# Two neighbouring up slots as one 2 MB transfer, with 16 KB in each partition

## The reference

```
logits = h @ w_router + b_router                # 32 experts, top 4 of each token
gates  = softmax(top values)
# for every block of rows that belong to one expert e:
gu   = xb @ w_up[e] + b_up[e]                   # w_up[e]: 1024 x 2048, 8 MB
gate = minimum(gu[:, :1024], 7);  up = clip(gu[:, 1024:], -7, 7)
act  = (up + 1) * (gate * sigmoid(1.702 * gate))
out  = act @ w_down[e] + b_down[e]              # w_down[e]: 1024 x 1024, 4 MB
y    = sum over the token's experts of gate weight * out
```

## Time and profile before

| | |
|---|---|
| time, median of 3 | 1277.09 us (1276.79 to 1278.07) |
| time of the profiled execution | 1276.55 us |
| its span, first to last instruction | 1274.8 us |
| granted TensorE clock, mean | 0.984 |
| PE busy | 1155.6 us (91%) |
| POOL busy | 650.7 us (51%) |
| DVE busy | 540.6 us (42%) |
| ACT busy | 242.6 us (19%) |
| HBM read | 447.00 MB, 353 GB/s over the span |

### The profile page before, as it was taken

The page is one execution under the profiler, slowest core; times in us unless marked ns, Lnnn a source line. Parts: engine busy times, 40 slices in busy tenths (PEclk is TensorE's granted clock), DMA queues, the critical chain, the costliest instruction groups (busy, mean ns, idle before and its releaser), DMA issues.

```text
span 1274.8 us, 30490 instructions
## 1 busy us (share of the span) xinstructions
PE 1155.6 (91%) x11113; PEld 578.5 (45%) x11114; DVE 540.6 (42%) x1161; ACT 242.6 (19%) x483; POOL 650.7 (51%) x743
## 2 busy tenths in 40 slices
PE   8999999999999889888898998998988889889886
PEld 7877777775434333333233433333333333333232
DVE  1999984122633233433332343332333233323424
ACT  2012124000222122122122221221212111222122
POOL 0022300000566766857862678577576765756863
PEclk9999999999999999999999999998999999999998
DMA  9983433642899999999998999999999999999993
GB/s 261 341 272 109 135 131 135 264 168 101 354 422 402 422 421 422 422 422 421 422 422 374 367 407 422 422 422 422 422 415 422 422 422 422 421 422 422 422 421 153
DMA packets 94581, 449.06 MB, mean 352 GB/s; under 512 B 8526, under 2 KB 42894, under 8 KB 45339
## 3 DMA queue, kind: packets, MB, share of 16 engines
q1 hardware_dynamic: 79918, 345.88, 68.1%
q0 software_dynamic: 13872, 101.52, 19.3%
q10 hardware_dynamic: 749, 1.19, 0.3%
HBM read 447.00 MB, written 2.42 MB: 353 GB/s over the span
## 4 chain that ended last, share of the span: by engine, by line
PE 41%; DMA 27%; DVE 13%; POOL 8%; issue 8%; POOLq 1%; ACT 1%; DVEq 0%; SPq 0%; ACTq 0%
DMA ring<-in_w_down 19%; PE banks L1392 13%; DVE arena L815 8%; DMA arena<-in_w_up 8%; PE banks L1405 8%; PE banks L1190 8%; POOL ring L526 7%; PE banks L1105 3%; PE banks L1306 2%; PE banks L1170 2%; PE banks L1142 2%; PE banks L1179 1%; PE banks L1149 1%; POOL ring L528 1%; DVE arena L824 1%
## 5 line engine op out<-in xcount | busy, mean ns | idle before, releaser
L1392 PE MATMUL banks<-ring,hT 128*32 128x512 f32 x3328 | 419.2, 603 | 44.6 <-POOL ring L528 32.9
L526 POOL COPY ring<-arena 128x1024 f32<-128x1024 f32 x279 | 291.2, 1044 | 129.8 <-POOLq L520 127.4
L528 POOL COPY ring<-arena 128x1024 f32<-128x1024 f32 x279 | 292.6, 1049 | 36.9 <-POOL ring L526 0.9
L1405 PE MATMUL banks<-ring,hT 128*32 128x256 f32 x3328 | 224.4, 389 | 45.2 <-DMA ring<-in_w_down 44.9
L345 DVE TENSOR_TENSOR xq<-xq,banks 128x256 f32<-128x256 f32 x53 | 22.3, 421 | 500.7 <-PE banks L1179 500.7
L1392 PEld LDWEIGHTS banks<-ring,hT 128*32 128x32 f32 x3328 | 98.2, 110 | 203.6 <-issue 96.4
L1190 PE MATMUL banks<-hT,ring 128*128 128x288 f32 x768 | 190.5, 409 | 0.0
L1405 PEld LDWEIGHTS banks<-ring,hT 128*32 128x32 f32 x3328 | 101.3, 111 | 185.8 <-issue 78.6
L532 POOL DMA_DIRECT2D ring<-in_w_down x96 | 50.8, 529 | 257.3 <-POOLq L520 142.6
L1190 PEld LDWEIGHTS banks<-hT,ring 128*128 128x128 f32 x768 | 146.4, 192 | 40.2
L783 DVE TENSOR_SCALAR WT<-slot_ids,prod 128x128 f32 x153 | 86.6, 622 | 62.3 <-PE banks L1105 62.0
(11 more groups left out here) (250 smaller groups left out, 817.1 us busy)
## 6 DMA issues: line engine op xcount, KB each, us to landing
arena<-in_w_up SPq DMA_DIRECT2D x248, 1024.0 KB, 14.1
ring<-in_w_down POOLq DMA_DIRECT2D x96, 1024.0 KB, 11.4
arena<-in_w_down SPq DMA_DIRECT2D x31, 1024.0 KB, 16.2
ring<-in_w_in SPq DMA_DIRECT2D x24, 1024.0 KB, 10.2
ring<-in_w_up SPq DMA_DIRECT2D x8, 1024.0 KB, 4.8
ring<-in_w_branch_b SPq DMA_DIRECT2D x4, 1024.0 KB, 4.9
ring<-in_w_branch_a SPq DMA_DIRECT2D x4, 1024.0 KB, 4.8
ring<-in_w_out SPq DMA_DIRECT2D x4, 1024.0 KB, 4.9
```

Of the source, the lines that this page charges most:

```text
L526: nc.gpsimd.tensor_copy(ring[:, k, 0:D], parked[k][:, 0:D]).then_inc(half_copied, 1)
L528: nc.gpsimd.tensor_copy(ring[:, k, D:SLOT], parked[k][:, D:SLOT]).then_inc(slot_full[k], 16)
L1392: ins = mm(UP[g * BLK:(g + 1) * BLK, :], xT[:, k, :], ring[:, k, g * 512:(g + 1) * 512], start=k == 0, stop=k == UP_SLOTS - 1)
L1405: ins = mm(DN[q * BLK:(q + 1) * BLK, 0:256], actT[:, f % 4, f // 4, :], ring[:, UP_SLOTS + j, h * D + q * 256:h * D + (q + 1) * 256], star ...
```

## The change

Up slots 2j and 2j+1 are loaded by one transfer. The 256 rows of w_up that they cover are dealt out so that partition p gets rows 2p and 2p+1, which are neighbours in HBM: 16 KB in one piece. Before, partition p of slot k got row p of its 128, 8 KB. The first row of each pair lies in the even slot, the second in the odd one. So the rows of the contraction that belong to an even slot are the even ones of the 256, and the token rows are turned by every second column (`pairs` in `turn_rows`). The norm weights are needed in this order too: a second copy of `norm_ffn_g` is loaded as four rows of 256, turned by two small transposes at the start into `pair_cols`, and used in `take_x`.

A pair has one semaphore, that of its even slot. SP loads a pair again when POOL has copied its odd slot. POOL's copies of both slots wait for the landing of the pair. The down slots are loaded as before.

```diff
+        def up_pair(e, k):
+            return a["w_up"][0, bass.ds(e, 1), k * P:(k + 2) * P, :].rearrange("e (p h) n -> p (e h n)", p=P)
...
-            def load_parked_again(place, after, ks):
-                for k in ks:
-                    sp.wait_ge(slot_full[k], place * 16 + 16 * FILLS)
-                    load_parked(after, k)
+            def load_parked_pair(e, k):
+                sp.dma_start(arena[:, k * SLOT:(k + 2) * SLOT], up_pair(e, k)).then_inc(parked_full[k], 16)
...
-            for k in range(EARLY_SLOTS):
-                load_parked(1, k)
-            for k in range(UP_SLOTS):
+            for k in (0, 2):
+                load_parked_pair(1, k)
+            for k in range(0, UP_SLOTS, 2):
                 sp.wait_ge(*mix_block_used(MIX_BLOCKS - SLOTS + k))
-                load_slot(0, k)
-                if k == 3:
-                    load_parked(1, EARLY_SLOTS)
+                sp.wait_ge(*mix_block_used(MIX_BLOCKS - SLOTS + k + 1))
+                load_pair(0, k)
+                if k == 2:
+                    load_parked_pair(1, 4)
...
             with sp.Fori(1, NE - 1) as place:
-                load_parked_again(place + 1, after, STAGED)
+                for k in range(0, UP_SLOTS, 2):
+                    sp.wait_ge(slot_full[k + 1], place * 16 + 16 * FILLS)
+                    load_parked_pair(after, k)
+                sp.wait_ge(slot_full[UP_SLOTS], place * 16 + 16 * (FILLS + 1))
+                load_parked(after, UP_SLOTS)
...
-                pool.wait_ge(parked_full[k], 16 * e)
+                pool.wait_ge(parked_full[k - k % 2 if k < UP_SLOTS else k], 16 * e)
...
+            act.dma_start(ws_region[0:4], a["norm_ffn_g"][0].rearrange("(j n) -> j n", j=4)).then_inc(vec_in, 16)
...
-                V.tensor_tensor(xT, XB[:, 256:512].rearrange("p (k t) -> p k t", k=KC),
-                                cols[:, NORM_FFN, :].unsqueeze(2).to_broadcast([P, KC, BLK]), ALU.mult
+                V.tensor_tensor(xT.rearrange("p (j h) t -> p j h t", h=2),
+                                XB[:, 256:512].rearrange("p (j h t) -> p j h t", j=4, h=2),
+                                pair_cols.unsqueeze(3).to_broadcast([P, 4, 2, BLK]), ALU.mult
...
-                    pe.wait_ge(vec_in, 16 * 8)
+                    pe.wait_ge(vec_in, 16 * 9)
+                    for h in range(2):
+                        tr(bank[7][:, 384 + 4 * h:388 + 4 * h], pair_rows[:, h])
...
+                pairs = xg.rearrange("t (p h) -> t h p", h=2)
                 for h in range(2):
-                    ins = tr(turned[:, h], xg[:, h * P:(h + 1) * P])
+                    ins = tr(turned[:, h], pairs[:, h])
...
             def up(k, fills):
-                pe.wait_ge(slot_full[k], fills)
+                pe.wait_ge(slot_full[k], fills - 16 * (k % 2))
```

More of the change, by code:

```diff
@@ L110, in hybrid_layer @@
         slot_ids = sb("slot_ids", [P, MAX_ROUNDS * BLK + BLK])
-        cols = sb("cols", [P, 8, KC])
+        cols = sb("cols", [P, 9, KC])
         bupT = sb("bupT", [P, NE, 2 * KC])
@@ L143, in hybrid_layer @@
         tmpc = region(2 * T).rearrange("p (h t) -> p h t", h=2)
-        WS = region(G * NS)[0:NS].rearrange("p (g i) -> p g i", g=G)
+        ws_region = region(G * NS)
+        WS = ws_region[0:NS].rearrange("p (g i) -> p g i", g=G)
+        pair_rows = ws_region[0:4].rearrange("j (p h) -> j h p", h=2)
         glu_tail = region(KC * NS).rearrange("p (c t) -> p c t", c=KC)
@@ L284, in hybrid_layer @@
         NORM_MIX, GATE_A, GATE_B, B_B, CONV_B, LNC_G, LNC_B, NORM_FFN = range(8)
+        pair_cols = cols[:, 8, :].rearrange("p (h j) -> p j h", h=2)
         vec_names = ["norm_mix_g", "b_gate_a", "b_gate_b", "b_branch_b", "conv_b", "ln_conv_g",
@@ L405, in load_slot, with load_pair @@
                 sp.dma_start(ring[:, k, :], weights(e, k)).then_inc(slot_full[k], 16)
+            def load_pair(e, k):
+                sp.dma_start(ring[:, k:k + 2, :].rearrange("p s n -> p (s n)"), up_pair(e, k)).then_inc(slot_full[k], 16)
             def load_parked(e, k):
                 sp.dma_start(parked[k], weights(e, k)).then_inc(parked_full[k], 16)
-            def load_parked_again(place, after, ks):
-                for k in ks:
-                    sp.wait_ge(slot_full[k], place * 16 + 16 * FILLS)
-                    load_parked(after, k)
+            def load_parked_pair(e, k):
+                sp.dma_start(arena[:, k * SLOT:(k + 2) * SLOT], up_pair(e, k)).then_inc(parked_full[k], 16)
             sp.wait_ge(sp_evac, 2 * G)
             sp.wait_ge(v_stored, 16)
-            for k in range(EARLY_SLOTS):
-                load_parked(1, k)
-            for k in range(UP_SLOTS):
+            for k in (0, 2):
+                load_parked_pair(1, k)
+            for k in range(0, UP_SLOTS, 2):
                 sp.wait_ge(*mix_block_used(MIX_BLOCKS - SLOTS + k))
-                load_slot(0, k)
-                if k == 3:
-                    load_parked(1, EARLY_SLOTS)
+                sp.wait_ge(*mix_block_used(MIX_BLOCKS - SLOTS + k + 1))
+                load_pair(0, k)
+                if k == 2:
+                    load_parked_pair(1, 4)
             sp.wait_ge(ya_evac, 2 * KC)
-            for k in range(EARLY_SLOTS + 1, PARKED - 1):
-                load_parked(1, k)
+            load_parked_pair(1, 6)
             sp.wait_ge(*mix_block_used(MIX_BLOCKS - SLOTS + UP_SLOTS))
             load_slot(0, UP_SLOTS)
-            load_parked(1, PARKED - 1)
+            load_parked(1, UP_SLOTS)
             sp.wait_ge(before_known, 1)
@@ L739, in _ @@
                     dve.wait_ge(pe_early, 1)
-                    V.tensor_copy(cols[:].rearrange("p v c -> p (v c)"), bank[7][:, 320:320 + 8 * KC]
+                    V.tensor_copy(cols[:].rearrange("p v c -> p (v c)"), bank[7][:, 320:320 + 9 * KC]
                                   ).then_inc(evac_early, 1)
```

## The result

| | before | after |
|---|---|---|
| time, median (lowest to highest) | 1276.94 us (1275.13 to 1278.07), 4 runs | 1319.91 us (1318.56 to 1321.28), 4 runs |
| ratio, 95% interval | | 1.0337 (1.0321 to 1.0353) |
| span of the profiled execution | 1274.8 us | 1317.4 us |

The change makes the kernel 43 us slower. The forecast was 54 us slower, 1331 us. The two spans differ by 42.6 us, and this is what the rest accounts for. Lines have moved: the up product is now L1410, the down product L1423, POOL's two half copies L539 and L541.

What follows compares the result with a forecast made beforehand. The prediction took the DMA engines to pace the expert loop, with PE waiting at the down product for slot 11's direct transfer. 1276.55 + 64.8 - 12.5 + 2.2 = 1331 us, range 1308 to 1345 (0.60); 8 in 10: 1282 to 1345.

Steps and rivals of the forecast that it cites:

- What bounds the kernel: Expert loop: DMA engines set the pace; PE waits 44.9 us at the down product for direct transfers, slot 11's last.
- The gain of a large piece: Up weights on SP's queue: 16 KB takes 611.7 ns against 621.2 for two of 8 KB, 0.30 us per expert.
- The loss of the other queue: POOL's direct transfers, in turn with 16 KB pieces, land 7.2 us later at nine places: 64.8 us.
- SP's queue doesn't run dry: During the direct transfers, SP's 4.4 MB open at 529 us and its next loads keep q1 busy over the 22 us.
- half of it: Rival: SP's queue runs dry in part of the nine places, 22 us slower, 1299 us (1284 to 1308); chance 0.13.
- The tenth place left out: Last long wait before the gap at 698 us: SP's open loads run out, so no 7.2 us counted there.
- What is given back: Short waits of 2.30 us at the down product, seven times, a body after the long ones, go: 12.5 us.
- The later issue: A pair's even slot is requested 2.2 us later: 2.2 us paid at the first reload, four other places taken at 0.
- The small parts: Strided turns, permuted output of `take_x` (0 to 4.4 us, taken at 0), and under 0.5 us at the start.
- The waits: Sign of being right: long waits of about 10 us at the down product and no short ones.
- The larger piece wins: Rival: engines share bytes evenly, 9.1 us off over 30 experts, 1272 us, 1267 at best; chance 0.12.
- Pieces of 8 KB: Rival: hardware cuts the pieces to 8 KB, leaving only the later issue, 1279 to 1290 us; chance 0.10.

Runs made afterwards that it cites:

- e12: Kernel before with slots 10 and 11 as one direct 2 MB transfer in 16 KB pieces, up slots still loaded singly in 8 KB pieces; 1273.18 us, ratio 0.9969.
- e1: Changed kernel with each 2 MB pair transfer in 8 KB pieces and the old order of rows; 1288.93 us, ratio 1.0085.
- e3: Kernel before with POOL's direct transfers cut into 4 KB pieces, SP's side untouched; 1340.3 us, ratio 1.05.
- e6: Changed kernel with SP's load of slot 8 cut into 4 KB pieces; 1294.54 us, ratio 1.0139.
- e10: Changed kernel's rows, but only slots 4 to 7 loaded as pairs in 16 KB pieces, slots 0 to 3 singly in 8 KB; 1310.79 us, ratio 1.0267.
- e8: Kernel before with the single loads of slots k and k+1 both issued after the copy of slot k+1; 1281.83 us, ratio 1.0043.
- e2: Kernel before with the changed order of rows alone, each up slot its own transfer in 8 KB pieces; 1281.34 us, ratio 1.0025.
- e7: Changed kernel with POOL's direct transfers of slots 9 to 11 moved earlier among its copies; 1371.3 us, ratio 1.0756.

## Why the prediction was right, and where its size was off

- **What bounds the kernel: right.** PE waits at the down product for the direct transfers, at nine places, and these places carry the loss (+49.4 of 42.6 us net). The pace of the DMA engines was close too: of 7.5 us of PE's waits taken away in e12, 3.5 to 4 came out in the time.
- **The gain of a large piece: right and small.** With pairs alone on the engines, 563 to 573 us, q1 moves 4.29 MB in 10 us, 429 GB/s. 16 x 16384 / 429 is 611 ns; the prediction had 611.7. Beside it, e1 from 557 to 567 us, 2 MB transfers in pieces of 8 KB, alone too: 422 GB/s, as with 1 MB before. So it is the piece that gains, not the transfer:

```profile
q1 hardware_dynamic: 297, 4.29, 100.8%
```

```profile
q1 hardware_dynamic: 547, 4.22, 101.3%
```

- **The loss of the other queue: right as a mechanism, its term mis-sized.** This is the one large term that was off. The prediction let all 24 direct pieces run against 16 KB pieces, 7.2 us. Only 16 do; eight meet slot 8, which stayed at 8 KB. 16 x 0.301 = 4.8 us, and the landings went from 16.1 to 20.9. Nine times that is 43.3 us instead of 64.8 (the nine landings grew by 43.7). The load was in the diff (`load_parked` for slot 8, issued at 539.09 us behind the pairs), and the prediction counted it in the open 4.4 MB without asking for its size. e3, where slot 8 has the larger piece too, gave +6.8 us per landing and 1340 us. e6 (slot 8 smaller still) and e10 (no pair behind slot 8) fit the same way of counting.
- **SP's queue doesn't run dry: right.** q1 and q0 are both busy up to the landing at 560 us; the next pair was issued in time, at 548.91. So the rival "half of it" falls: the loss per place is two thirds of what was forecast, but at all nine places, and by the size of slot 8's pieces.
- **The tenth place left out: right, nearly.** Its landing came 1.9 us later (15.9 to 17.8), its body grew by 1.2 us.
- **What is given back: right for six of the seven short waits.** -12.5 us were forecast; the bodies of the six are 13.4 us shorter. They stand two bodies behind a long one. The seventh, 1.3 us in the body at 356, has no long wait ahead of it and was wrongly counted with them: its own direct transfer meets large pieces too (17.9 us instead of 15.2), and the body grew by 3.3 us. The DMA engines are at 325 GB/s in the fourth body of the group and at 397 in the loop, under 400 as forecast. That the group of five bodies takes 94.1 us against the forecast 94 is luck: +7.2 and -2.3 were forecast, +5.9, +1.1, +0.4 and -2.5 came.
- **A term not seen: the clock.** The prediction has no term for it. Of the nine bodies' +49.4 us, 6.3 lie behind the landing. In the four where the clock was full before, the rest of the body behind the landing took 2.0 us, and it takes 3.4 to 3.5 now. In three of the nine (778, 867 and 958) the clock had been low in that place before too; there the rest did not grow, and these three grew least (+4.0 to +4.9). In the two left (1015 and 1196) it had been low in part, and the rest grew by 0.8 and 1.0. So the 6.3 us go with the clock; no kernel was made that changes it alone. The mean granted clock fell from 0.984 to 0.958; at the lower level it counts half, so 1317.4 x 0.042 x 2 = 111 us are spent there, against 1274.8 x 0.016 x 2 = 41 before.

```profile
core 0: 1317.4 us, clock 0.958
```

- **The later issue: under-priced as a mechanism, hidden in this kernel.** SP's first reload was issued at 337.91 instead of 335.20 us, 2.7 us later where 2.2 were forecast. But PE's bodies at 340 and 356 began only 0.5 and 0.6 us later than before, so no run shows the 2.2 us as time of its own. "Taken at 0" at four places holds where PE sets the pace. Once the large pieces are taken away, the later issue costs 5 us by itself (e8).
- **The small parts: not quite nothing.** 3 us for the rows (e2); whether the kernel after pays them was not shown.
- **The waits.** "Long waits of about 10 us" came as two of 4.5 and 2.2 us. The first is at slot 10, because it too arrives late; its product and an up slot behind it then fill part of the gap.
- **The larger piece wins:** fell (429 against 422 GB/s, and 43 us lost). The Trainium skill ("DMA: Bandwidth & Descriptors", section "Rules for kernel authors") asks for transfers of at least 1 MiB. Here they are 1 MB before, and 2 MB in the same pieces brought nothing (422 GB/s in e1), so above 1 MB the trace shows no gain from the size of a transfer. **Pieces of 8 KB:** fell by the queue view (3.15 against 1.57 MB in equal packets), and e1 shows what it would have been, 1289 us, inside the 1279 to 1290 given for it.

With the mis-sized term put right, the prediction's own sum is 1276.55 + 43.3 - 12.5 + 2.2 = 1309.5 us. To this come 0.4 for the landings as measured, 6.3 behind them and -0.6 ahead of them, 3.3 for the body at 356, 1.2 for the tenth, -0.9 more given back, 0.1 for the bodies at a lower clock (+3.4 and -3.3), and -0.2, since everything else came to 2.0 us and not 2.2. That makes 1319.1 us; the profiled execution took 1318.99. So part of the forecast's closeness is luck: a term 21.5 us too large stood against some 10 us of terms that it did not have.

Open: what in the new rows costs e2's 3 us; how much the common landing costs by itself; the clock's 6.3 us, which were read from the traces and not tested.

## What to carry to other kernels

When two DMA queues shared the engines here, the size of the piece in a partition set their shares (3.15 against 1.57 MB at 16 and 8 KB): enlarging it on the queue that isn't late took bandwidth from the one that is. Before making a transfer larger, find the transfer that the bottleneck engine waits for, list what is open on the other queue piece by piece while it is under way (each load with its own size, not the queue's typical one), and sum piece by piece in turn. The cheap lever is the other way round: give the late queue the larger pieces, and stop when the other side begins to be waited for. Here that was worth 0.3% (e12).

## What was not expected of the hardware

- The granted clock after a wait of PE. Behind waits of 4.5 and 2.2 us it was 0.54 from 557 to 567 us, and sixteen down matmuls took 1.93 us where they take 1.07. Behind the single wait of 3.04 us the kernel before had stayed at full speed, as its window from 547 to 557 us shows:

```profile
547.00:557.00 10.00, 9.72 (x110) 3.90 (x105) 3.73 (x10) 3.22 (x7) 4.76 (x5) 1.00 1.01 421
```

- It did not stay there at every place. The kernel before was granted 0.89 and 0.92 in the bodies at 867 and 958, each with a long wait of 3.2 and 3.1 us. In the nine bodies it was granted 0.89 to 1.00, the kernel after 0.79 to 0.91.
- 0.54 is the lower of the two levels (1.2 GHz) in nearly all of that stretch. Across most of the kernels the mean clock goes down as the waits at the down product add up: 0.984 before (44.9 us) and in e12 (37.4), 0.979 in e1 (54.0), 0.970 in e6 (55.3), 0.958 after (68.9), 0.953 in e3 (91.6). e7 has 0.979, with 29.9 us there and 99.0 at the copies, so the sum of the waits is not all of it. A stall costs more than its length: 6.3 + 3.4 - 3.3 us over nine places, 0.7 us more for each than in the kernel before.
- The turn between queues is by single pieces and close to exact: 208 packets against 208 at sizes of 16 and 8 KB, 163 against 167 at even sizes, 526 against 526 at 8 and 4 KB. In four stretches of 0.3 us from 541.0 us on, q0 of the kernel after starts 8, 6, 2 and 8 packets. That is a wave of 0.9 us, the time of one 8 KB and one 16 KB piece; turns of several pieces would make it longer.

```profile
q0 software_dynamic: 8, 0.07, 52.3%
q0 software_dynamic: 6, 0.05, 39.5%
q0 software_dynamic: 2, 0.02, 12.9%
q0 software_dynamic: 8, 0.07, 52.2%
```
